# First modulation group by column halves in a hybrid attention, RWKV-7, HGRN2 and MoE step

## The reference

```python
h = rms_norm(x, p['norm_mix_g']) * (1.0 + scale1) + shift1
proj = h @ p['w_in']                      # 1024 x 3200
mod = silu(c) @ w_mod + b_mod             # 1024 x 6144
shift1, scale1, gate1, shift2, scale2, gate2 = split(mod, 6)
```

## Time and profile before

| | us |
|---|---|
| median of 3 runs | 1215.68 |
| lowest and highest | 1212.77, 1220.65 |
| the profiled execution, its own time | 1215.87 |
| its span in the trace | 1214.2 |
| TensorE busy | 1151.8 (95% of the span) |
| VectorE busy | 331.4 |
| ScalarE busy | 213.3 |
| moved by DMA | 458.91 MB, 378 GB/s on average |

### The profile page before, as it was taken

One profiled execution on the slowest core, in us unless ns is written; L12 is line 12 of the kernel. 1 busy time (PEld: TensorE's weight loads), 2 busy tenths in 40 slices (PEclk: granted clock), 3 DMA queues, 4 the chain that ended last, 5 costly groups with the idle time before them and its releaser, 6 DMA issues.

```text
span 1214.2 us, 17161 instructions
## 1 busy us (share of the span) xinstructions
PE 1151.8 (95%) x7144; PEld 466.4 (38%) x7144; DVE 331.4 (27%) x682; ACT 213.3 (18%) x381; POOL 44.9 (4%) x77
## 2 busy tenths in 40 slices
PE   4998999889999999999999999999999999999996
PEld 0534577765333333333333333333333333333332
DVE  1202877844312211112211221111221122111112
ACT  1212264422111111111111111111111111111112
POOL 0310200000000000000000000000000000000000
PEclk9999999999999999999999999999999999999998
DMA  9999300499999999999999999999999999999994
GB/s 380 307 361 370 119 2 4 149 351 414 394 426 431 430 430 431 429 432 430 432 431 432 430 432 430 431 432 432 430 432 431 432 431 432 429 432 431 432 431 205
DMA packets 44511, 458.91 MB, mean 378 GB/s; under 512 B 5301, under 2 KB 7517, under 8 KB 16689
## 3 DMA queue, kind: packets, MB, share of 16 engines
q1 hardware_dynamic: 41328, 451.46, 88.2%
q0 software_dynamic: 2656, 5.67, 1.6%
q10 hardware_dynamic: 480, 1.13, 0.2%
HBM read 456.76 MB, written 1.47 MB: 377 GB/s over the span
## 4 chain that ended last, share of the span: by engine, by line
PE 86%; DMA 6%; DVE 4%; issue 2%; SPq 1%; ACT 1%; another core or an unknown queue 0%; DVEq 0%; ACTq 0%
PE bank L1311 35%; PE bank L1334 18%; PE bank L658 7%; PE bank L1269 5%; PE bank L1253 4%; DMA ring<-in_moe_w_gu_dram 4%; PE bank L1291 3%; PE bank L1068 2%; DMA ring<-in_w_mod_dram 2%; DVE const_sb L2280 2%; PE bank L1261 2%; PE bank L633 1%; PE bank L646 1%; PE bank L778 1%; SPq L414 1%
## 5 line engine op out<-in xcount | busy, mean ns | idle before, releaser
L1311 PE MATMUL bank<-ring,proj 128*64 128x512 f32 x1024 | 226.7, 593 | 6.3 <-DMA ring<-in_moe_w_gu_dram 6.2
L2271 DVE TENSOR_SCALAR const_sb<-bank 128x512 f32<-128x512 f32 x32 | 22.1, 692 | 417.9 <-PE bank L1311 417.9
L1311 PEld LDWEIGHTS bank<-ring,proj 128*64 128x64 f32 x1024 | 72.6, 137 | 155.7 <-issue 139.9
L1334 PE MATMUL bank<-ring,const_sb 128*64 128x512 f32 x512 | 116.9, 599 | 4.8 <-DVE const_sb L2280 4.8
L1334 PE MATMUL bank<-param_sb,const_sb 128*64 128x512 f32 x512 | 116.9, 599 | 4.8 <-DVE const_sb L2280 4.8
L1697 ACT ACTIVATE const_sb<-const_sb 128x512 f32<-128x512 f32 x32 | 20.2, 630 | 568.6 <-DVE const_sb L2271 568.6
L1311 PE MATMUL bank<-proj 128*64 128x512 f32 x512 | 115.3, 592 | 0.0
L2285 DVE TENSOR_TENSOR x_res<-bank,x_res 128x512 f32<-128x512 f32 x64 | 41.2, 686 | 246.7 <-PE bank L1334 246.7
L658 PE MATMUL bank<-ring,param_sb 128*128 128x512 f32 (+2 forms) x224 | 88.3, 550 | 0.0
L1311 PEld LDWEIGHTS bank<-proj 128*64 128x64 f32 x512 | 36.8, 137 | 73.1 <-issue 73.1
L1269 PE MATMUL bank<-x_res,const_sb 64*128 64x512 f32 x256 | 63.6, 615 | 0.9 <-DVE x_res L2285 0.9
(11 more groups left out here) (361 smaller groups left out, 948.4 us busy)
## 6 DMA issues: line engine op xcount, KB each, us to landing
ring<-in_moe_w_gu_dram SPq DMA_DIRECT2D x64, 2048.0 KB, 34.4
proj<-in_moe_w_gu_dram SPq DMA_DIRECT2D x32, 2048.0 KB, 32.2
ring<-in_moe_w_down_dram SPq DMA_DIRECT2D x32, 2048.0 KB, 30.9
param_sb<-in_moe_w_down_dram SPq DMA_DIRECT2D x32, 2048.0 KB, 32.5
spare<-in_moe_w_gu_dram SPq DMA_DIRECT2D x16, 2048.0 KB, 30.0
const_sb<-in_moe_w_gu_dram SPq DMA_DIRECT2D x16, 2048.0 KB, 31.6
ring<-in_w_mod_dram SPq DMA_DIRECT2D x12, 2048.0 KB, 13.9
ring<-in_w_in_dram SPq DMA_DIRECT2D x5, 2048.0 KB, 12.4
```

The source lines that it names most:

```text
L1311: mm = pe.matmul(b[CAP * half:CAP * half + CAP, :], xT[:, k % 4, k // 4, :], w[:, 2048 * kc + o + 512 * half:2048 * kc + o + 512 * half + ...
L1334: mm = pe.matmul(b_down[CAP * half:CAP * half + CAP, :], aT[:, k % 4, k // 4, :], w[:, D * kc + 512 * half:D * kc + 512 * half + 512], sta ...
L2271: ts(moe["glu"], b_glu[:, :], LIMIT, None, ALU.min).then_inc(sem("glu_sb"), 1)
```

## The change

The four pieces of the first modulation group are cut otherwise. Piece `mod0 k` is now half `k // 2` of the columns of shift1 and of scale1 (512 of 1024 each) and half `k % 2` of the contraction, loaded in two transfers of 1 MB with runs of 512 columns; `modulation0(part)` multiplies 256 columns at a time, and adding b_mod, turning, and scaling x are done for each part. A part of the columns of shift1 and scale1 is a half of the contraction of the projections. `project` takes a range of chunks: the four products of pieces 0 and 1 do the first four chunks ("upper") after part 0 and the last four after part 1, with `modulation0(1)` between (1,0) and (1,1) and the turn of part 1 in the middle of (1,1). The weights of pieces 0 and 1 are loaded in two halves (`in_upper`, `in`). x goes on SP's queue behind `mod0 0`; its transposes go in front of the modulation, and the part of them that waits is copied out of PSUM at once and scaled in place later. `FRONT` has another order and three more places (`spare`, and the ring slots 4 and 5 once more), and each entry names what frees its place. GpSimd's norm_ffn_g load waits for the second turned part, and the constants of the mixers for `mod 2` instead of `mod 3`. b_mod comes in six transfers instead of two. The numbers of `mod_sb` go up by one. Left out of the diff below are lines with such a number alone and unchanged lines.

```diff
@@ -43,16 +43,21 @@
-FRONT = [("mod0", 0, 0), ("mod0", 1, 1), ("mod0", 2, 4), ("mod0", 3, 5), ("in", 0, 0), ("in", 1, 1), ("mod", 0, 4),
-         ("in", 2, 0), ("mod", 1, 5), ("in", 3, 1), ("mod", 2, 4), ("mod", 3, 5), ("in", 4, 0), ("mod", 4, 4), ("mod", 5, 5),
-         ("in", 5, 1), ("mod", 6, 4), ("mod", 7, 5), ("in", 6, 0), ("out", 0, 4), ("out", 1, 3)]
-FRONT_ROUNDS = [sum(slot == j for _, _, slot in FRONT) for j in range(NSLOT)]
+SPARE = NSLOT
+FRONT = [("mod0", 0, 0, None), ("x", 0, None, None), ("mod0", 1, 1, None), ("in_upper", 0, SPARE + 1, None), ("in_upper", 1, SPARE + 2, None),
+         ("mod0", 2, SPARE, None), ("mod0", 3, 0, ("mod", 1)), ("in", 0, 4, None), ("in", 1, 5, None), ("in", 2, 1, ("mod", 2)),
+         ("mod", 0, SPARE, ("mod", 3)), ("in", 3, 0, ("mod", 4)), ("mod", 1, 4, ("proj", 0)), ("mod", 2, 5, ("proj", 1)),
+         ("in", 4, SPARE, ("mod", 5)), ("in", 5, 1, ("proj", 2)), ("mod", 3, 4, ("mod", 6)), ("mod", 4, 5, ("mod", 7)),
+         ("mod", 5, 4, ("mod", 8)), ("in", 6, 0, ("proj", 3)), ("mod", 6, 5, ("mod", 9)), ("mod", 7, 4, ("mod", 10)),
+         ("out", 0, 4, None), ("out", 1, 3, None)]
+LOADS = {"mod0": 2, "mod": 1, "in_upper": 1, "in": 1, "out": 1, "x": 0}
+FRONT_ROUNDS = [sum(LOADS[kind] for kind, _, slot, _ in FRONT if slot == j) for j in range(NSLOT + 3)]
...
-for kind, k, slot in FRONT:
-    FRONT_AT[kind, k] = (slot, 1 + sum(s == slot for _, _, s in FRONT[:FRONT.index((kind, k, slot))]))
+for at_, (kind, k, slot, _) in enumerate(FRONT):
+    FRONT_AT[kind, k] = (slot, sum(LOADS[name] for name, _, s, _ in FRONT[:at_ + 1] if s == slot))
@@ -132,8 +137,7 @@
-    jobs = [("cT",), ("modT",)]
-    jobs += [("xT", s, h) for s in range(2) for h in range(2)]
+    jobs = [("cT",)] + [("xT", s, h) for h in range(2) for s in range(2)] + [("modT", 0)]
@@ -314,12 +318,14 @@
+        front = [ring[:, j, :] for j in range(NSLOT)] + [spare[:, :], ring[:, 4, :], ring[:, 5, :]]
+        front_full = ring_full + [sem("home_full0"), sem("home_full1"), sem("home_full7")]
...
-        ring_of = {2: 0, 3: 1, 4: 2, 5: 5, 8: 3, 9: 4}
-        home_full = [ring_full[ring_of[j]] if j in ring_of else sem(f"home_full{j}") for j in range(NHOME)]
-        home_used = [ring_used[ring_of[j]] if j in ring_of else sem(f"home_used{j}") for j in range(NHOME)]
+        ring_of = {0: SPARE, 1: SPARE + 1, 7: SPARE + 2, 2: 0, 3: 1, 4: 2, 5: 5, 8: 3, 9: 4}
+        home_full = [front_full[ring_of[j]] if j in ring_of else sem(f"home_full{j}") for j in range(NHOME)]
+        home_used = [ring_used[ring_of[j]] if ring_of.get(j, SPARE) < NSLOT else sem(f"home_used{j}") for j in range(NHOME)]
@@ -417,29 +423,38 @@
-            for kind, k, slot in FRONT:
+            for kind, k, slot, freed in FRONT:
+                if freed and freed[0] == "mod":
+                    sp.wait_ge(sem("mod_used"), freed[1])
+                if freed and freed[0] == "proj":
+                    name = ("proj", freed[1], 1)
+                    sp.wait_ge(full[jobs[name] % ROT], jobs[name] // ROT + 1)
+                if kind == "x":
+                    for s, name in enumerate(("x_prompt", "x_sample")):
+                        sp.dma_start(x[:, s, :], a[name][0]).then_inc(sem("x_in"), 16)
...
-                    ring_load(slot, w_mod[:, 2 * k:2 * k + 2, 0:2048])
-                if kind == "in":
-                    if k < 2:
-                        sp.wait_ge(sem("mod_used"), 1 + k)
-                    else:
-                        name = ("proj", k - 2, 1)
-                        sp.wait_ge(full[jobs[name] % ROT], jobs[name] // ROT + 1)
+                    part, j = k // 2, k % 2
+                    for g in range(2):
+                        sp.dma_start(front[slot][:, 2048 * g:2048 * g + 2048].rearrange("p (c n) -> p c n", c=4),
+                                     w_mod[:, 4 * j:4 * j + 4, D * g + 512 * part:D * g + 512 * part + 512]).then_inc(front_full[slot], 16)
+                if kind in ("in_upper", "in"):
...
-                    ring_load(slot, w_in[:, :, lo:lo + w])
+                    c = slice(0, 4) if kind == "in_upper" else slice(4, KC) if k < 2 else slice(0, KC)
+                    sp.dma_start(front[slot][:, c.start * w:c.stop * w].rearrange("p (c n) -> p c n", n=w), w_in[:, c, lo:lo + w]) \
+                        .then_inc(front_full[slot], 16)
...
-                    sp.wait_ge(sem("mod_used"), 3 + k)
...
-                    ring_load(slot, w_mod[:, 2 * j:2 * j + 2, 2048 * g:2048 * (g + 1)])
+                    sp.dma_start(front[slot].rearrange("p (c n) -> p c n", c=2), w_mod[:, 2 * j:2 * j + 2, 2048 * g:2048 * (g + 1)]) \
+                        .then_inc(front_full[slot], 16)
...
             for g in (1, 2):
-                sp.wait_ge(sem("mod_sb"), g + 1)
+                sp.wait_ge(sem("mod_sb"), g + 2)
...
+            sp.wait_ge(full[jobs["proj", 4, 1] % ROT], jobs["proj", 4, 1] // ROT + 1)
@@ -522,10 +537,14 @@
-            bsrc = a["b_mod"][0].rearrange("(g q n) -> q g n", g=3, q=4)
             for s in range(2):
-                pool.dma_start(mod_sb[s:s + 97:32], bsrc).then_inc(sem("bmod_in"), 16)
-            after(pool, "modT")
+                for g in range(2):
+                    pool.dma_start(mod_sb[s + 64 * g:s + 64 * g + 33:32, 0, :].rearrange("q (part n) -> q part n", part=2),
+                                   a["b_mod"][0][D * g:D * g + D].rearrange("(part q n) -> q part n", part=2, q=2)).then_inc(sem("bmod_in"), 16)
+            bsrc = a["b_mod"][0][2 * D:].rearrange("(g q n) -> q g n", g=2, q=4)
+            for s in range(2):
+                pool.dma_start(mod_sb[s:s + 97:32, 1:3, :], bsrc).then_inc(sem("bmod_in"), 16)
+            after(pool, "modT", 1)
@@ -551,7 +570,7 @@
-            slot, times = FRONT_AT["mod", 3]
+            slot, times = FRONT_AT["mod", 2]
@@ -620,20 +639,39 @@
-                pe.wait_ge(ring_full[slot], 16 * times)
+                pe.wait_ge(front_full[slot], 16 * times)
...
-            def modulation(kind, j):
...
-                b = bank[6 if kind == "mod" and j < 4 else 7]
-                slot = loaded(kind, j)
+            c_silu = keep["c_silu"].rearrange("p (c m) -> p c m", m=32)
...
+            def modulation(j):
...
+                b = bank[6 if j < 4 else 7]
+                slot = loaded("mod", j)
...
                     for q in range(4):
-                        mm = pe.matmul(b[32 * q:32 * q + 32, :], keep["c_silu"].rearrange("p (c m) -> p c m", m=32)[:, k],
-                                       ring[:, slot, kc * 2048 + q * 512:kc * 2048 + (q + 1) * 512],
+                        mm = pe.matmul(b[32 * q:32 * q + 32, :], c_silu[:, k],
+                                       front[slot][:, kc * 2048 + q * 512:kc * 2048 + (q + 1) * 512],
...
+            def modulation0(part):
...
+                for j in range(2):
+                    w = front[loaded("mod0", 2 * part + j)].rearrange("p (g c n) -> p g c n", g=2, c=4)
+                    for kc in range(4):
+                        k = 4 * j + kc
+                        for q in range(4):
+                            mm = pe.matmul(bank[7 - part][32 * q:32 * q + 32, 0:256], c_silu[:, k],
+                                           w[:, q // 2, kc, 256 * (q % 2):256 * (q % 2) + 256],
+                                           start=(k == 0), stop=(k == KC - 1), skip_group_check=True)
+                    mm.then_inc(sem("mod_used"), 1)
...
+            def turn_mod0(part):
...
+                pe.wait_ge(sem("mod_sb"), part + 1)
+                transposes(("modT", part), [mod_sb[:, 0, 256 * part + P * c:256 * part + P * c + P] for c in range(2)])
@@ -647,16 +685,17 @@
-            def project(n, s):
-                lo, w = PIECES[n]
-                slot = loaded("in", n)
-                wv = ring[:, slot, 0:KC * w].rearrange("p (c n) -> p c n", n=w)
-                b = open_bank(pe, "proj", n, s)
-                for c in range(KC):
+            def project(n, s, lo=0, hi=KC):
+                w = PIECES[n][1]
+                slot = loaded("in_upper" if hi <= 4 else "in", n)
+                wv = front[slot][:, 0:KC * w].rearrange("p (c n) -> p c n", n=w)
+                b = bank[jobs["proj", n, s] % ROT] if lo else open_bank(pe, "proj", n, s)
+                for c in range(lo, hi):
...
-                filled(mm, "proj", n, s)
+                if hi == KC:
+                    filled(mm, "proj", n, s)
@@ -1076,41 +1115,46 @@
-            for j in range(4):
-                modulation("mod0", j)
-            pe.wait_ge(sem("mod_sb"), 1)
-            transposes(("modT",), [mod_sb[:, 0, P * c:P * (c + 1)] for c in range(4)])
-            for s in range(2):
-                pe.wait_ge(sem("x_norm"), s + 1)
-                for part in range(2):
+            for part in range(2):
+                for s in range(2):
+                    pe.wait_ge(sem("x_norm"), s + 1)
...
-            project(0, 0)
-            project(0, 1)
-            project(1, 0)
```

(100 more changed lines are left out.)

6 lines of the change are left out of this document (3 added, 3 removed).

## The result

| | us |
|---|---|
| kernel before, median of 20 runs | 1211.81 |
| changed kernel, median of 20 runs | 1222.74 |
| ratio | 1.0081, 95% interval 1.0068 to 1.0094 |
| profiled execution of the changed kernel, its own time and span | 1220.13, 1218.4 |
| forecast and range | 1219.2, 1210 to 1225 |

The change costs 0.8%, some 9.8 us by the ratio. The direction and the range held; the size is three times what I had worked out, and only partly for the reason that I had given. The two profiled executions lie 4.3 us apart and the medians 10.9: the one of the kernel before took 4.1 us more than its median, the one of the changed kernel 2.6 us less.

What follows compares the result with a forecast made beforehand. The front was bound by the first group's weights and GpSimd's small loads, later stages by DMA streaming. Gate products at the later of 101.6 and 105.5, against 102.21, add 3.3 to 1215.87: 1219.2 us, range 1210 to 1225.

Steps and rivals of the forecast that it cites:

- x and its norm, the first half: Front: x landed at 11.7, transposes from 16.4, high clock at about 22, first modulation half ended at 24.5 us.
- The turn: Between first modulation half and projections: 2.1 us, all idle; projections at 26.6 instead of 34.4, modulation 0 at 58.0.
- rival 3: Clock stays low in the front or falls in the 2.1 us turn: 3 us later everywhere, 1222.4 or 1226; chance 0.14.
- SP's order: SP's queue: `in 5` waits ahead of `mod 3`, which lands at 89.5; TensorE wants it at 84.9, stall 4.6 us.
- GpSimd's string: Small loads wait for the second turned half: norm_ffn at 43.3, constants at 87.2, last router_w half landed at 105.1.
- my lower bound: If the constants need no room from the load before them, they go at 80.6 and the end is 98.5.
- a sign of being wrong: The forecast would be wrong if GpSimd issued the constants before 82 us.
- rival 2: Constants issued at 81 share engines with `in 5` and `mod 3`, moved to about 94; total 1217.9 us; chance 0.12.
- Where the gate products wait: They start at the later of 101.6 (TensorE) and 105.5 (router_w), against 102.21: 3.3 us later.
- The price of a hole in clock: Low clock behind the stall at modulation 3 costs 1.7 to 3.4 us, taken as 2.3.
- Packets: Modulation pieces in 2 KB runs, not 8: 1.5 us of queue, hidden by TensorE except 0.3 on x.
- The base: The sum started from the kernel before's profiled 1215.87 us: span 1214.2 and 1.7 around it.

Runs made afterwards that it cites:

- second profile: Another profiled execution of each kernel, nothing edited: kernel before, span 1212.7 us; changed kernel, span 1218.6 us.
- the turn covered: Changed kernel with `mod 3` ahead of `in 5`, norm_ffn_g behind the parameter rows, x's upper-half transposes behind the first modulation half; ratio to kernel before 1.0031.
- constants after `mod 3`: Changed kernel, but the constants of the mixers wait for `mod 3` again instead of `mod 2`; ratio to the kernel before 1.0108.

## Why the prediction was right and wrong

- **x and its norm, the first half.** x at 11.7 forecast, landed at 12.11; the 0.7 us of the slowest engine in it was my estimate: in the kernel before, SP's queue had moved the four pieces (8.4 MB) by some 25.7 us and the last counted as landed at 26.34, 0.6 us later, and no run shows which engine was last. Transposes at 16.4 forecast, 16.89 measured; the half ended at 24.5, measured 24.36. The half-width products cost what the columns cost (64 in 3.89 us, two old pieces 3.84). Right. The high level from about 22 us was my estimate too, and no run shows it: the granted clock reads 1.00 all the way from 16 to 24 us. What the trace shows in its place is the length of the records: 16 transposes in 3.65 us (1.91 in the second profile of the kernel before), then 24 records of the half in 1.73 us (72 ns each) and the other 40 in 2.16 (54 ns).
- **The turn.** 2.1 us forecast, 2.4 measured, projections at 26.75 (26.6). What failed is the clock behind it: I put a drop in the turn into rival 3 and out of the sum. It fell (0.50 granted over 28 to 31 us), and 12.23 us stand where 10.3 were forecast (10.54 at a granted 1.00, with the turn covered). Modulation 0 thus began at 60.1 instead of 58.0, 1.7 us ahead of the kernel before and not 3.9 (0.8 against its second profile, 60.87).
- **SP's order.** The stall ahead of modulation 3, behind an empty stretch of the queue, was found from the diff and is there. Its size was 4.6, measured 9.41 and 6.65. Without the constants beside it, it is 3.81. The term was right for the case that I took, and the case was wrong: the constants go beside `mod 3`. `mod 3` landed at 96.6 and 93.9, where I had 89.5.
- **GpSimd's string.** Here a step failed. "Constants at 79.6 + 7.6 = 87.2" rested on the belief that they need the room of the load ahead of them. They do not: they leave 0.8 us behind it in both profiles. In the first that was 80.85, close to my lower bound (80.6) and under the 82 that I had named as a sign of being wrong. In the second it was 85.60, near my 87.2, but only because the load ahead of them stood until 84.82 (by the same shift of 7.6 I had it at 79.9). From there to the landing of the last router_w half it was 21.0 and 21.5 us where I took 17.9: the first half of router_w waits too (4.6 and 4.7 us; in the kernel before it went out at 85.37, right behind the constants). The start of the string was right in kind (behind the second turned half), 2 us later in size. Other issues of the string do stand until an earlier load lands, in the kernel before at 43.03, 72.26 and 96.06 against landings at 42.7, 71.9 and 95.7; that room is what they lack was my reading of it.
- **The constants beside `in 5` and `mod 3`.** This is rival 2, to which I gave 0.12. It had `mod 3` at about 94 and 1217.9 us; measured 96.6 and 93.9. That the queues share, and that GpSimd's with its 16 KB packets gets most of the bytes and `in 5` with its 2 KB the least, is what the trace shows: 82 packets with 1.34 MB against 83 with 0.36 MB from 86 to 90 us, and 86 with 1.41 MB against 88 with 0.70 MB from 92 to 97 us in the second profile, where SP's are those of `mod 3`. `in 5` took 12.8 us to land in the first profile, and 8.1 in the second, in which it was through before the constants flowed.
- **Where the gate products wait.** I had them wait for router_w, at 105.5. In the first profile they started at 107.7 without a hole, since the one before had already cost more, and router_w had landed at 101.8. In the second they waited for router_w, landed at 107.1, as forecast. I had compared the two as a maximum, which was the right form: with either wait taken away the other, or the low clock behind it, still held TensorE.
- **The price of a hole in clock.** Forecast 2.3 us behind the hole, between half of 3.4 and half of 6.8 us at the low level. These are (1 - 0.83) x 2 x 10 and (1 - 0.60) x 2 x 8.5 in the two windows of the earlier trace rows, with a low level of 0.50 (granted over 27 to 33 us in the kernel before). Measured: modulation 3 took 3.33 instead of 1.92 (0.50 granted over 96 to 99 us), and the product behind it ran at the high clock (7.13 us, 1.00 over 100 to 107): 1.4 us. In the second profile it was 3.64, and the product took 8.07 instead of 7.13: 2.7 us. But the sum ended on the router_w term, so this one did not enter it.
- **Packets.** 1.5 us of queue, hidden, by the row. No run here isolates it.
- **The base.** I summed against one profiled execution. It was 4 us above the kernel's median, and its hole (3.60) and its low clock behind it (I took 1.8 us, the rows give 1.5) did not stand in the second profile. The sum of 3.3 us was measured from there; from the second profile's 99.6 it would have been 5.9, and 7.4 with the low clock that I expected. So the forecast of the time was in part lucky: the base was 4.1 us too high by the medians and the step 7.6 us too small, and 3.5 us of error were left.

## What to carry to other kernels

Where a queue of transfers is issued in a fixed order, look at each entry for the moment when its place comes free, and put no entry that must wait ahead of one that need not. When two waits in a row end within a few us of each other, an experiment that takes one away shows nothing; take away both before calling either harmless. Ask of a large load in long runs what lies beside it: here the constants took 3.7 times the bytes of the transfer that TensorE waited for. And before summing against a profile, see how far its own time lies from the median: here the same hole was 3.6 us in one execution and 2.0 in the next, and in the changed kernel 9.4 and 6.7.

## What the runs showed of the hardware that I had not expected

- Two queues with work on the same engines sent about the same number of packets, though of other sizes: 82 and 83 from 86 to 90 us, with 1.34 and 0.36 MB (changed kernel, first profile), 86 and 88 from 92 to 97 us, with 1.41 and 0.70 MB (second).
- A gap of 1.96 us on TensorE left the clock at its high level (second profile of the kernel before, 1.00 granted over 97 to 107 us), and one of 2.80 us did too (covered turn, 1.00 over the same). One of 2.4 us with 0.4 us of transposes in it (the turn) was followed by the low level in six of the seven profiles of kernels that have it (0.50 to 0.68 granted over 28 to 31 us): three upper halves in 12.23 us. In the seventh (constants after `mod 3`) the granted clock stayed at 1.00 and they took 10.54, but the modulation half ahead of the turn had taken 4.56 instead of 3.7 to 4.0. With the turn covered it was 1.00 and 10.54 again, and 5.47 and 4.62 for the half. No run shows what decides.
- In a kernel that is not changed at all, one load of GpSimd's string took 2.6 us to land in one execution and 6.4 in the next, issued 1.0 us later, and the loads behind it moved by 4.75 us.
